# Hybrid decoder layer on one core: a ring of two difference buffers in the HGRN2 scan, and another order of the work at the scan's first chunk

## The reference

```python
def mixer(h):
    hq, hf, hi, hg, gqkv, gz, ga, gb = split(h @ w_in)
    f = lb + (1 - lb) * sigmoid(hf)
    o_a = hgrn2_chunked(silu(hq), 1 - f, hi, log(f))       # 4 heads
    ...
    o_b = gated_delta_chunked(gq, gk, gv, log_a, beta)     # 4 heads
    return concat(rms_norm(o_a) * silu(hg), rms_norm(o_b) * silu(gz)) @ w_out

def hgrn2_step(state, q, k, v, b):       # b: cumulative sum of log f within the chunk
    scores[t, s] = sum_d q[t, d] * k[s, d] * exp(b[t, d] - b[s, d])     # s <= t
    o = scores @ v + (q * exp(b)) @ state
    state = exp(b_last) * state + (k * exp(b_last - b)).T @ v
```

## Time and profile before

| | |
|---|---|
| median of three runs | 1446.57 us (1445.41 to 1448.29) |
| profiled execution | 1448.29 us, span 1446.6 us, 19612 instructions |
| TensorE busy | 1411.8 us (98% of the span) |
| VectorE, ScalarE, GpSimd busy | 1024.3, 709.6, 232.5 us |
| granted TensorE clock, mean | 0.997 |
| scan | about 432 to 580 us |
| chain that ended last | 93% TensorE, 3% VectorE, 2% ScalarE, 1% transfers |

### The profile page before, as it was taken

One profiled execution on the slowest core, in us unless ns is written; L12 is line 12 of the kernel. 1 busy time (PEld: TensorE's weight loads), 2 busy tenths in 40 slices (PEclk: granted clock), 3 DMA queues, 4 the chain that ended last, 5 costly groups with the idle time before them and its releaser, 6 DMA issues.

```text
span 1446.6 us, 19612 instructions
## 1 busy us (share of the span) xinstructions
PE 1411.8 (98%) x7167; PEld 1184.5 (82%) x7167; DVE 1024.3 (71%) x1511; ACT 709.6 (49%) x1302; POOL 232.5 (16%) x243
## 2 busy tenths in 40 slices
PE   5999999999999999999999999999999999999996
PEld 4877888878889999888888888888888888888885
DVE  5666445643128888367897999999999575677566
ACT  5432467422238888357674444434445444454434
POOL 3000001001019777010000000000000245311010
PEclk9999999999999999999999999999999999999998
DMA  8563414554614333444442334334327755324222
GB/s 217 86 109 44 35 61 120 158 123 102 153 34 135 118 118 101 176 144 148 140 147 77 111 115 157 113 101 162 116 88 256 244 191 195 126 73 146 80 97 101
DMA packets 156318, 181.52 MB, mean 125 GB/s; under 512 B 21240, under 2 KB 96190, under 8 KB 156222
## 3 DMA queue, kind: packets, MB, share of 16 engines
q1 hardware_dynamic: 155968, 180.16, 43.0%
q10 hardware_dynamic: 254, 0.10, 0.0%
HBM read 130.95 MB, written 49.28 MB: 125 GB/s over the span
## 4 chain that ended last, share of the span: by engine, by line
PE 93%; DVE 3%; ACT 2%; DMA 1%; issue 1%; SPq 0%; POOL 0%; ACTq 0%; DVEq 0%; POOLq 0%
PE psum L2305 10%; PE psum L2307 10%; PE psum L2306 10%; PE psum L566 5%; PE psum L568 5%; PE psum L567 5%; PE psum L2244 4%; PE psum L2245 4%; PE psum L2246 4%; PE psum L2217 4%; PE psum L2219 4%; PE psum L2218 4%; PE psum L1229 4%; PE psum L621 3%; PE psum L623 3%; PE psum L622 3%
## 5 line engine op out<-in xcount | busy, mean ns | idle before, releaser
L150 DVE TENSOR_TENSOR w_wlo<-w_raw,w_whi 128x1024 fp32r<-128x1024 f32 x70 | 94.0, 1342 | 251.0 <-ACT w_whi L144 250.7
L144 ACT ACTIVATE w_whi<-w_raw 128x1024 fp32r<-128x1024 f32 x70 | 74.0, 1057 | 184.5 <-PE psum L2219 85.4
L2305 PE MATMUL psum<-m_hi,w_whi 128*128 128x512 f32 x416 | 162.4, 390 | 1.5 <-issue 0.7
L2307 PE MATMUL psum<-m_hi,w_wlo 128*128 128x512 f32 x416 | 161.9, 389 | 0.0
L2306 PE MATMUL psum<-m_lo,w_whi 128*128 128x512 f32 x416 | 161.9, 389 | 0.0
L566 PE MATMUL psum<-h_hi,w_whi 128*128 128x512 f32 x320 | 127.0, 397 | 3.7 <-DVE h_lo L853 3.7
L568 PE MATMUL psum<-h_hi,w_wlo 128*128 128x512 f32 x320 | 125.6, 393 | 0.0
L567 PE MATMUL psum<-h_lo,w_whi 128*128 128x512 f32 x320 | 125.6, 392 | 0.0
L2244 PE MATMUL psum<-w_whi,g_slot 128*128 128x512 f32 x308 | 120.1, 390 | 0.6 <-DVE w_wlo L3021 0.6
L2245 PE MATMUL psum<-w_wlo,g_slot 128*128 128x512 f32 x308 | 119.8, 389 | 0.0
L2246 PE MATMUL psum<-w_whi,g_slot 128*128 128x512 f32 x308 | 119.8, 389 | 0.0
(11 more groups left out here) (377 smaller groups left out, 3450.8 us busy)
## 6 DMA issues: line engine op xcount, KB each, us to landing
w_raw<-in_w_up SPq DMA_DIRECT2D x39, 512.0 KB, 3.9
w_raw<-in_w_in SPq DMA_DIRECT2D x36, 512.0 KB, 6.5
s_rows<-pair_work SPq DMA_DIRECT2D x11, 1024.0 KB, 4.1
w_raw<-s_rows SPq DMA_DIRECT2D x44, 256.0 KB, 2.6
g_rows<-pair_work SPq DMA_DIRECT2D x18, 512.0 KB, 2.6
w_raw<-g_rows SPq DMA_DIRECT2D x33, 256.0 KB, 3.1
w_raw<-in_w_out SPq DMA_DIRECT2D x16, 512.0 KB, 4.2
mixed_home<-in_w_down SPq DMA_DIRECT2D x32, 256.0 KB, 3.4
```

Of the source, the lines that this page charges most:

```text
L2305: pe.matmul(out, wh[:, part], hi(kt), start=(start and kt == 0), stop=False)
L2307: ins = pe.matmul(out, wl[:, part], hi(kt), start=False, stop=(stop and kt == KT // 2 - 1))
```

## The change

The ring of `ed` has two buffers in place of three, so the difference of level n waits for GpSimd's level n-2. Chunk 0 loses most of its special order: before it only levels 0 to 2 get differences and exponentials (behind the silu of the last head's first half, not ahead of it), and only levels 0 and 1 get GpSimd's products; levels 3 to 5 take the places that they have in every other chunk. TensorE's first solve comes ahead of score 1. The rounding and remainder of one slab move from the end of chunk 0 to its start, VectorE's behind two memsets and ahead of the placing of score 1. The late silu moves from behind the first `act_vn` to the end of chunk 0. Exponential 3 of chunk 0 follows `act_vn`. The space that is reserved for descriptors of transfers grows from 1024 to 2048 bytes a partition; with one `ed` buffer of 2048 bytes less, addresses of tensors shift.

```diff
-        self.ed = [c(f"s_h_ed{i}", [P, DG]) for i in range(3)]
+        self.ed = [c(f"s_h_ed{i}", [P, DG]) for i in range(2)]
...
@@ Front.act
-        for lv in range(3):
-            self.scan.act_exp(act, 0, lv)
         act.wait_ge(s["summed"], NH)
         self.act_last(act, 0, ACT.Silu)
-        for lv in range(3, 6):
-            self.scan.act_exp(act, 0, lv)
+        self.scan.act_exp(act, 0, 0)
+        self.scan.act_exp(act, 0, 1)
+        self.scan.act_exp(act, 0, 2)
         self.act_last(act, 1, ACT.Copy)
...
@@ Scan.pe
         self.pe_score(pe, 0, 0)
+        self.pe_solve(pe, 0)
         self.pe_score(pe, 0, 1)
-        self.pe_solve(pe, 0)
...
@@ Scan.act
         self.act_vn(act, 0)
-        self.front.act_late_silu(act)
+        self.act_exp(act, 0, 3)
         self.act_last_decay(act, 0)
+        self.slabs.round(act, self.front.first["q"] + NH + 1, self.multiplied)
         for c in range(NT):
...
+            self.act_exp(act, c, 4)
             if c:
-                self.act_exp(act, c, 4)
                 self.act_root(act, c - 1)
-                self.act_exp(act, c, 5)
+            self.act_exp(act, c, 5)
...
-            else:
-                self.slabs.round(act, self.front.first["q"] + NH + 1, self.multiplied)
...
             self.act_squares(act, c, 0)
+            if c == 0:
+                self.front.act_late_silu(act)
...
@@ Scan.dve_differ
-        if n >= 3:
-            dve.wait_ge(self.s["levels"], n - 2)
+        if n >= 2:
+            dve.wait_ge(self.s["levels"], n - 1)
...
@@ Scan.dve
-        for lv in range(6):
-            self.dve_differ(dve, 0, lv)
+        self.dve_differ(dve, 0, 0)
+        self.dve_differ(dve, 0, 1)
+        self.dve_differ(dve, 0, 2)
...
-            if c:
-                self.dve_differ(dve, c, 3)
+            self.dve_differ(dve, c, 3)
             self.dve_place(dve, c, 0)
             if c == 0:
                 dve.memset(self.state[:], 0.0)
                 dve.memset(self.hstate[:], 0.0).then_inc(s["cleared"], 1)
+                self.slabs.remainder(dve, self.front.first["q"] + NH + 1)
                 dve.wait_ge(s["cleared"], 2)
...
             self.dve_place(dve, c, 1)
+            self.dve_differ(dve, c, 4)
             if c:
-                self.dve_differ(dve, c, 4)
                 self.dve_rhs(dve, c)
             self.dve_place(dve, c, 2)
+            self.dve_differ(dve, c, 5)
             if c:
-                self.dve_differ(dve, c, 5)
                 self.dve_dt(dve, c, 1)
...
-            else:
-                self.slabs.remainder(dve, self.front.first["q"] + NH + 1)
...
@@ Scan.pool (both loops ahead of chunk 0)
-        for lv in range(3):
+        for lv in range(2):
...
-                if c or lv > 2:
+                if (c, lv) not in ((0, 0), (0, 1)):
                     self.pool_level(pool, c, lv)
...
@@ kernel
-    nc = bacc.Bacc("TRN2", target_bir_lowering=False, num_devices=1, dynamic_dma_scratch_size=1024)
+    nc = bacc.Bacc("TRN2", target_bir_lowering=False, num_devices=1, dynamic_dma_scratch_size=2048)
```

More of the change, by code:

```diff
@@ L1411, in act_exp @@
         for side, sign in ((0, -1.0), (1, 1.0)):
-            here = self.front.level_view(self.ed[(c * LEVELS + lv) % 3][:], m, side)
+            here = self.front.level_view(self.ed[(c * LEVELS + lv) % 2][:], m, side)
             ins = act.activation(here, here, ACT.Exp, scale=sign)
@@ L1551, in dve_differ @@
         n = c * LEVELS + lv
-        if n >= 3:
-            dve.wait_ge(self.s["levels"], n - 2)
+        if n >= 2:
+            dve.wait_ge(self.s["levels"], n - 1)
         b = self.part(self.front.f, c).rearrange("p h (n m) -> p h n m", m=2 * m)
         middle = b[:, :, :, m - 1:m].broadcast_to([P, NH, P // (2 * m), 2 * m])
-        out = heads(self.ed[n % 3][:]).rearrange("p h (n m) -> p h n m", m=2 * m)
+        out = heads(self.ed[n % 2][:]).rearrange("p h (n m) -> p h n m", m=2 * m)
         dve.tensor_tensor(out, b, middle, ALU.subtract).then_inc(self.s["differed"], 1)
@@ L1704, in pool_level @@
             pool.tensor_tensor(self.blocks(heads(self.kl[n % 3][:]), m, 0), self.blocks(self.part(self.front.kk, c), m, 0),
-                               self.blocks(heads(self.ed[n % 3][:]), m, 0), ALU.mult)
+                               self.blocks(heads(self.ed[n % 2][:]), m, 0), ALU.mult)
         if 1 in sides:
             pool.tensor_tensor(self.packed_blocks(self.ql[n % 3][:], m), self.blocks(self.part(self.front.q, c), m, 1),
-                               self.blocks(heads(self.ed[n % 3][:]), m, 1), ALU.mult).then_inc(s["levels"], 1)
+                               self.blocks(heads(self.ed[n % 2][:]), m, 1), ALU.mult).then_inc(s["levels"], 1)
     def pool_query(self, pool, c):
```

## The result

The changed kernel takes 1454.88 us (median of four runs, 1453.76 to 1455.27), the kernel before 1446.9 us beside it: ratio 1.0053, 95% interval [1.0041, 1.0066]. It is 8.0 us slower. The forecast was slower by 3.2 us, 1449.8 us, with a range up to 1452.8: the sign was right, the size was not, and the time lies outside the range.

A forecast was written before the change was run, and what follows sets the result against it. TensorE's instruction queue, busy 98% of the span, was taken as the bound. Its delay at chunk 1's product of vn and kd (+3.7-0.6, chunk 0's 1.9 inside) was taken as +3.2 us on 1446.57: 1449.8 us, range 1446.2 to 1452.8.

The forecast's parts named there:

- ring of two: Steady chunks: level 6's difference waits some 0.2 us once a chunk, hidden by VectorE's slack; taken at 0, bounds 0 and 1.2.
- 2.8 us late, and score 7 and the matmuls behind it with it: Chunk 0: placing of score 3 frees the bank of lt and x at 444.0 against 441.18, delaying the matmuls behind.
- The remainder and the missing early differences: Front of chunk 0: remainder of 1.5 us holds VectorE to 439.0, level 4 comes at 442.55; score 5 stalls 2.6 us.
- What comes back (0.9 us): Near the end of chunk 0, TensorE's waits for placing x (0.2 us) and the hgrn state (0.7) go: credit 0.9.
- The late silu (+3.7-0.6): Chunk 1: exponential 5 starts at 461.1, 3.7 us late behind the silu and table loads; 0.6 of that is slack.
- The early exponentials and the solve: Before and in early chunk 0: 0.1 us left, vn copy wait of 0.8 stays; solve priced 0, bounds -0.3 and +0.2.
- The rule on shared ports: Chunk 0: remainder waits for GpSimd's q product, starting at 438.05; VectorE free at 439.3, not 439.0; sum would be +3.5.
- A: Rival: the change costs as worked out in chunks 0 and 1, +2.0 to +4.5 us, 1449.8; chance 0.54.
- B: Rival: blocked VectorE costs less, level 4 in time or more slack in chunk 1; 1447.6 us; chance 0.24.
- C: Rival: the two-buffer ring binds in every chunk, 0.3 to 1 us in seven chunks; 1453.8 us; chance 0.13.
- D: Rival: faster, larger scratch lets SP's transfers be issued sooner at the start; 1443.8 us if 6 gained; chance 0.05.

The follow-up runs named there:

- experiment 1: Changed kernel with nine filler products of constants in TensorE's queue ahead of score 5 of chunk 0: 1452.45 us, 1.0037 of the kernel before.
- experiment 14: Changed kernel with three difference buffers, scratch of 1024 bytes and fourteen filler products ahead of score 5 of chunk 0: 1450.97 us, 1.0032 of the kernel before.
- experiments 6: Kernel before with only the slab's rounding and remainder moved to the start of chunk 0, early differences kept: 1452.09 us, 1.0039 of the kernel before.
- experiment 9: Kernel before with the slab's rounding and remainder at the start of chunk 0, plus eleven filler products ahead of score 5: 1449.52 us, 1.0014.
- experiment 13: Changed kernel with nine fillers ahead of score 5 and, in chunk 0, the copy of y ahead of exponential 1 of chunk 1: 1452.29 us, 1.0042.
- experiment 3: Changed kernel with three difference buffers and 1024 bytes of scratch again, order as changed: 1454.82 us, 1.0051 of the kernel before.
- experiment 2: Changed kernel with the slab's rounding and remainder back at their old place, the end of chunk 0: 1453.44 us, 1.0044 of the kernel before.
- experiment 10: Changed kernel with the late silu at the end of chunk 2 instead of chunk 0: 1454.48 us, 1.0052 of the kernel before.
- experiment 4: Kernel before with only the descriptor scratch raised from 1024 to 2048 bytes: 1447.23 against 1446.93 us, 1.0001.
- 8: Changed kernel, ring of two kept, with the slab moved to chunk 3 and the late silu to the end of chunk 2: 1452.37 us, 1.004.
- experiment 5: Kernel before with only the late silu moved to the end of chunk 0: 1449.34 us, 1.002 of the kernel before.
- 7: Changed kernel with three difference buffers, the slab in chunk 3 and the late silu at the end of chunk 2: 1452.15 us, 1.0031.

## Why the prediction was wrong, step by step

The scan's delay of 6.8 us parts as follows, from the changed kernel and experiments 1 and 14. The last column has the differences of medians.

| part | forecast | in the scan | between medians |
|---|---|---|---|
| order of chunks 0 and 1, clock held, three buffers | 3.2, with two waits of the ring in it | 3.1 | 4.6 |
| ring of two, clock held | 0 beyond that (0 to 1.2) | 2.2 | 0.9 to 1.3 |
| TensorE's clock | not in the sum | 1.5 | 2.4 |
| sum | 3.2 | 6.8 | 8.0 |

The clock's part between medians is clear of noise: the runs of experiments 6 and 9 don't overlap, and those of experiment 1 and of the changed kernel do so in one run only. The ring's part is not, and the scans carry the 0.7 us named above. That 3.1 meets 3.2 is partly luck: the forecast followed the ring's waits for differences 2 and 6 in chunk 0, and the 3.1 is of a kernel without them.

- **The step that failed: "2.8 us late, and score 7 and the matmuls behind it with it".** It took a stall for a pure shift: behind it every matmul, by this step, takes its old time. No term of the sum was for the clock. Shown otherwise: behind idle stretches of 1.94 and 0.67 us the granted clock was 0.50 from 444 to 450 us. Experiment 1 fills the idle time, holds the clock and wins 2.4 us; experiment 9 does the same to another version and wins 2.6. The Trainium skill, "TensorE: Matmul & The Clock Gate", section "The HAM clock gate", says that the clock drops from 2.4 to 1.2 GHz after idle time and comes back only after sustained work. The 0.50 at 94 to 100% busy agrees with that for the way back. On how much idle time brings the fall the page and these runs differ, and the runs decide: 1.94 and 0.67 us were enough here. The forecast should have had it as a rival: with the 1.5 to 2.4 us that the runs show for it, the sum of 3.2 would have been 4.7 to 5.6. That is still short of 8.0.
- **The ring of two, taken at 0: followed in part in chunk 0, and missed where it cost most.** In the steady chunks the step was right: level 6's difference starts 0.04 us after GpSimd's level 4 there, the later chunk still takes 19.04 us, and chunks 2 to 7 lose 0.3 us. But there ScalarE, VectorE and GpSimd have slack; in chunk 0 the levels run late, and VectorE waits 1.31 and then 0.95 us. The first of these waits was in the forecast's path to 444.0; the second, for difference 1 of chunk 1, was not. It makes exponential 1 late, behind which the copy of y is queued, and TensorE waits 0.94 us for that copy once the clock is held. ScalarE reaches the late silu 1.8 us later than with three buffers (454.13-430.82 = 23.3 us after score 0 in experiment 13, 452.69-431.19 = 21.5 in 14), and the four table loads stand behind it. The ring measured 2.2 us in the scan, 0.9 to 1.3 between medians. Ahead of score 5 it makes TensorE late as well (the wait for `s_g_rn`), which the late level 4 covers: with three buffers TensorE waits 3.45 us there (experiment 3), with two 1.94, and score 5 starts at about the same time.
- **The remainder and the missing early differences: right where they were followed, 0.3 to 0.5 us short once counted from score 0, but one cause was credited with both.** The remainder took 1.23 us, not the 1.5 taken. By experiment 2 the remainder delays score 5 by 1.5 us (10.7 against 9.15 after score 0), and the lost early differences with the ring by 1.3 (9.15 against 7.8). TensorE's wait was 1.94 and not 2.6 us since it came to score 5 later itself.
- **What comes back (0.9 us)**: the waits for the state and for x did go. With the clock held the wait for the copy of y (0.94 us in experiment 1) takes as much again, and it was not foreseen.
- **The late silu (+3.7-0.6)**: exponential 5 of chunk 1 started at 464.00, forecast 461.1; nearly all of the 2.9 us is what ScalarE was late before it (the table load at 456.71 against 453.9). The chain itself was right: 7.3 us from that load to exponential 5, forecast 7.2. Waits for normed (0.39) and score 6 (0.40) came as named. Taken alone, with some of the clock in it, the silu costs 2.5 us; at the end of chunk 2 it costs 1.2 us in the scan (experiment 10).
- **The early exponentials and the solve**: the wait for vn stayed, at 0.65 against 0.8 us, but nothing was gained: the solve had waited 0.47 us for `s_g_rn`, and score 2 starts 4.3 us after score 0, before 3.7 (436.04-431.76 and 435.86-432.12). The forecast had 0.1 us gained and a bound of +0.2 for the solve. With three buffers both waits are gone (experiment 14).
- **The rule on shared ports**: the Trainium skill, "SBUF — State Buffer", section "Who interferes with whom", had the remainder wait for GpSimd's product. GpSimd waited instead: its q product has 1.72 us from 437.68, the remainder 1.23 from 437.58, since the remainder had started first. That the two exclude each other agrees; it cost TensorE nothing, for level 4 waited for the exponential. In experiment 14 GpSimd's product started first, at 435.80, and there the remainder of 435.84 took 1.75 us.
- **Rivals.** A named the waits, but even with the clock held the kernel is 5.5 us above before (experiment 1), outside A's +2.0 to +4.5. B is refuted, no slack took up the waits. C had nearly the right time (1453.8) for the wrong reason: the ring did not bind in every chunk. D is refuted by experiment 4.
- **Open**: for the order alone the scan shows 3.1 us and the medians 4.6. Against experiment 4's scan of 145.9 it would be 3.8; the rest lies within the scatter of the front and the intervals of the medians, and I can't part it further. What decides whether the clock falls behind waits of 0.8 and 0.7 us isn't known: it fell in experiment 2 and not in 8. Nor is it behind a longer one: behind 1.21 us it fell in experiment 5 and not in 14.

## What to carry to other kernels

Where one engine is the bound and TensorE is that engine, an idle stretch of 2 us can cost more than 2 us: look for rows of PEclk below 1.00 with PE busy right behind a wait, and try a few filler products in the wait, which shows how much of a loss is the clock. Price a smaller ring in the chunk where the pipeline is behind, not in the steady ones where its wait is hidden. A piece of work moved to a later chunk is not a piece removed: look for its cost there, as the silu showed. And where a wait is taken away from a chain with a late engine, look for it again at the next instruction that this engine feeds, as the copy of y showed.

## What the runs showed of the hardware

In the profiled executions the granted clock fell behind stretches with these idle times of TensorE ahead, in us: 1.94 and 0.67 (changed kernel, experiment 10), 0.83 and 0.67 (experiment 2), 1.21 (experiment 5), 2.7 and 0.7 (6), 1.77 (7), and within a single wait of 3.45 (3). It did not fall with 0.82 and 0.67 (8), with 0.67 and 0.94 (1), behind a single wait of 1.21 (14), nor behind one of 1.17 late in chunk 1 (3). So up to about 1.2 us the length of the wait alone does not tell; in every kernel that waited 1.77 us or more ahead of score 5 it fell. It stayed low for 3 to 10 us (3 in experiment 2, 7 in the changed kernel, 10 in experiment 3). While it was low, eight matmuls of 128x128 took 2.02 us and not 1.11. The prediction had none of it, with TensorE busy for 98% of the span. The fillers, matmuls of no use, held the clock at 1.00 in all five kernels that had them.
